# Summing three modulation parts on VectorE in the down stage of the first layer, in a two-layer hybrid decoder trunk

## What is computed

```
c_act = silu(c)
for l in range(2):
    mod = c_act @ ada_w[l] + ada_b[l]              # 1024 x 6144 weights, one row of c
    sh1, sc1, gt1, sh2, sc2, gt2 = split(mod, 6)   # parts 0, 1, 2, 3, 4, 5
    h = rms_norm(x, norm1_g[l]) * (1 + sc1) + sh1
    x = x + gt1 * token_mixer(h, ...)
    h = rms_norm(x, norm2_g[l]) * (1 + sc2) + sh2
    x = x + gt2 * conv_gated_mlp(h, ...)
return rms_norm(x, final_g)
```

## Time and profile before

| what | value |
|---|---|
| median of 3 runs | 1051.32 us (1051.12 to 1051.36) |
| the profiled execution | 1051.65 us, its span 1049.9 us |
| TensorE clock granted, mean | 0.982 |
| busy: PE, DVE, ACT | 94%, 72%, 50% of the span |
| chain that ended last | PE 67%, DVE 17%, issue 10% |
| read from HBM | 199.83 MB, 191 GB/s over the span |

### The profile page before, as it was taken

The page is one execution under the profiler, slowest core; times in us unless marked ns, Lnnn a source line. Parts: engine busy times, 40 slices in busy tenths (PEclk is TensorE's granted clock), DMA queues, the critical chain, the costliest instruction groups (busy, mean ns, idle before and its releaser), DMA issues.

```text
span 1049.9 us, 20436 instructions
## 1 busy us (share of the span) xinstructions
PE 989.0 (94%) x7817; PEld 919.1 (88%) x7817; DVE 751.8 (72%) x1127; ACT 524.6 (50%) x733; POOL 18.0 (2%) x23
## 2 busy tenths in 40 slices
PE   3599999989999999999999999988999999999997
PEld 2498899879888999989898999888988989999997
DVE  2438889996495788876345698999567678788733
ACT  2555355538334555654345544654743466555532
POOL 5000000000000000000000000000000000000001
PEclk8799999999999999999999999999999999999999
DMA  8865545536695354966763545544667635555551
GB/s 303 290 201 163 175 147 183 173 106 214 228 345 177 126 194 163 340 241 240 274 207 98 160 136 170 187 139 153 201 241 279 214 129 183 161 189 173 174 188 41
DMA packets 138952, 202.25 MB, mean 193 GB/s; under 512 B 3416, under 2 KB 114148, under 8 KB 138852
## 3 DMA queue, kind: packets, MB, share of 16 engines
q1 hardware_dynamic: 138501, 200.68, 56.8%
q10 hardware_dynamic: 351, 0.21, 0.1%
HBM read 199.83 MB, written 1.05 MB: 191 GB/s over the span
## 4 chain that ended last, share of the span: by engine, by line
PE 67%; DVE 17%; issue 10%; DMA 2%; SPq 2%; ACT 2%; DVEq 1%; ACTq 0%
PE PB L1280 15%; PE PB L1282 14%; PE PB L1281 14%; DVE wL L862 5%; DVE buf L951 4%; PE SC L1280 2%; PE SC L1281 2%; PE SC L1282 2%; PE MI L1231 2%; DMA raw<-in_w_in 2%; PE PB L1303 1%; DVE rdev L1009 1%; PE ST L1333 1%; DVE cb L1097 1%; PE PB L1304 1%
## 5 line engine op out<-in xcount | busy, mean ns | idle before, releaser
L862 DVE TENSOR_TENSOR wL<-raw,wH 128x2048 fp32r<-128x2048 f32 (+3 forms) x152 | 322.8, 2125 | 120.5 <-ACT wH L606 118.5
L1280 PE MATMUL PB<-hH,wH 128*128 128x256 f32 x1376 | 397.9, 289 | 9.1 <-DVE wL L862 9.1
L1281 PE MATMUL PB<-hL,wH 128*128 128x256 f32 x1376 | 390.6, 284 | 0.0
L1282 PE MATMUL PB<-hH,wL 128*128 128x256 f32 x1376 | 390.5, 284 | 0.0
L606 ACT ACTIVATE wH<-raw 128x2048 fp32r<-128x2048 f32 (+3 forms) x152 | 268.2, 1782 | 121.9 <-DMA raw<-in_w_down 57.8
L1280 PEld LDWEIGHTS PB<-hH,wH 128*128 128x128 f32 x1376 | 265.0, 193 | 24.3 <-issue 13.9
L1281 PEld LDWEIGHTS PB<-hL,wH 128*128 128x128 f32 x1376 | 265.1, 193 | 0.9 <-issue 0.7
L1282 PEld LDWEIGHTS PB<-hH,wL 128*128 128x128 f32 x1376 | 265.2, 193 | 0.0
L951 DVE SCALAR_TENSOR_TENSOR buf<-G,vec,buf 128x256 f32<-128x256 f32 x240 | 98.0, 477 | 0.3
L1303 PE MATMUL PB<-hH,wH 128*128 128x256 f32 x192 | 57.4, 299 | 15.1 <-DVE hL L879 12.3
L1097 DVE SCALAR_TENSOR_TENSOR cb<-PB,vec,cb 128x255 f32<-128x255 f32 (+1 forms) x88 | 36.3, 476 | 32.2 <-ACT cb L753 32.2
(11 more groups left out here) (256 smaller groups left out, 1706.2 us busy)
## 6 DMA issues: line engine op xcount, KB each, us to landing
raw<-in_w_in SPq DMA_DIRECT2D x48, 1024.0 KB, 5.3
raw<-in_w_up SPq DMA_DIRECT2D x44, 1024.0 KB, 5.1
ada<-in_ada_w SPq DMA_DIRECT2D x40, 1024.0 KB, 7.5
raw<-in_w_down SPq DMA_DIRECT2D x22, 1024.0 KB, 4.9
ada_pre<-in_ada_w SPq DMA_DIRECT2D x8, 1024.0 KB, 12.1
raw<-in_w_o SPq DMA_DIRECT2D x8, 1024.0 KB, 8.3
raw<-in_w_out_diff SPq DMA_DIRECT2D x4, 1024.0 KB, 5.1
raw<-in_w_out_conv SPq DMA_DIRECT2D x4, 1024.0 KB, 6.3
```

Of the source, the lines that this page charges most:

```text
L862: dve.tensor_tensor(wL[s][:, 0:size], raw[s][:, 0:size], wH[s][:, 0:size].bitcast(F32), ALU.subtract).then_inc(w_lo[s], 1)
L1280: pe.matmul(out, a, xh(k), start=first and k == 0, stop=False, skip_group_check=True)
L1281: pe.matmul(out, a, xl(k), start=False, stop=False, skip_group_check=True)
L1282: ins = pe.matmul(out, b, xh(k), start=False, stop=last and k == kt - 1, skip_group_check=True)
```

## The change

Three parts of layer 1 (0, 1 and 3) are no longer made by PE's steps. In layer 0's down stage SP loads their twelve chunks (`SUM_LOADS`), DVE multiplies each half of a chunk (128 x 1024) by its scalar of `c_col` and adds it to an accumulator of 128 x 1024 (`ada_sums` at `SUM_STEPS`, 24 instructions, each waiting for the one before), and PE sums over the partitions by eight matmuls with the accumulator as weights and two columns of ones (`reduce_sums`, after chunks 69, 72, 74). ACT has no copy in this. Two accumulators lie over `ca`, `cb` and `th`, `gy`. PE's steps after chunks 61 to 64, 67 to 69 and 71 of layer 0 go, and so do those after 14, 18, 23, 27 of layer 1 with the reduction after 29; in layer 0 these last stay, now under an `If`. The four loads of part 2 of layer 1 stood at steps 71, 72, 73 and 75 of SP; now all stand at step 75, each behind a wait for a sum of DVE that frees its buffer, and ahead of SP's loads of layer 1's first chunks.

```
-ADA_PARTS = [2, 3, 4, 5, 0, 1]
-ADA_GAP, ADA_NEXT, ADA_CHUNKS = 12, 16, 24
-ADA_STEPS = [1, 4, 7, 10, 14, 18, 23, 27, 31, 33, 35, 37] + [None] * 4 + [61, 62, 63, 64, 67, 68, 69, 71]
-ADA_LOADS = [n + 1 for n in ADA_STEPS[:ADA_GAP]] + [39, 40, 42, 41] + [59, 60, 61, 62, 65, 66, 67, 69] + [71, 72, 73, 75]
-ADA_REDUCE_AT = {12: 0, 29: 1, 39: 2, UP + 4 * UP_LOOPS: 3, 65: 4, 73: 5}
+ADA_PARTS = [2, 3, 4, 5]
+ADA_ONCE, ADA_GAP, ADA_CHUNKS = 8, 12, 16
+ADA_STEPS = [1, 4, 7, 10, 14, 18, 23, 27, 31, 33, 35, 37] + [None] * 4
+ADA_LOADS = [n + 1 for n in ADA_STEPS[:ADA_GAP]] + [39, 40, 42, 41]
+ADA_REDUCE_AT = {12: 0, 29: 1, 39: 2, UP + 4 * UP_LOOPS: 3}
+SUM_PARTS = [0, 1, 3]
+SUM_STEPS = [66, 67, 67, 68, 69, 70, 70, 71, 72, 73, 73, 73]
+SUM_LOADS = [59, 60, 61, 62, 70, 71, 71, 72, 73, 74, 74, 75]
+SUM_BUF = [1, 2, 3, 0] * 3
+SUM_REDUCE_AT = {69: 0, 72: 1, 74: 2}
...
+        sums = [ups[:, i:i + 2, :, :].rearrange("p a k t -> p (a k t)") for i in (0, 2)]
...
             def load_ada(l, a):
...
+                if a < ADA_CHUNKS:
+                    sp.wait_ge(ada_used, ADA_FIRST + l * 12 + (a if a < ADA_GAP else a - 3))
+                else:
+                    sp.wait_ge(ada_sum, 2 * (a - ADA_CHUNKS + 9))
...
+            def load_sum(b):
+                part, i = SUM_PARTS[b // ADA_PART], b % ADA_PART
+                if b < ADA_PART:
+                    sp.wait_ge(ada_used, ADA_FIRST + ADA_GAP + b + 1)
+                else:
+                    sp.wait_ge(ada_sum, 2 * (b - 3))
...
+                if n in SUM_LOADS:
+                    with sp.If(l < LAYERS - 1):
+                        for b in range(len(SUM_LOADS)):
+                            if SUM_LOADS[b] == n:
+                                load_sum(b)
+                        if n == CHUNKS - 1:
+                            for i in range(ADA_PART):
+                                load_ada(l, ADA_CHUNKS + i)
...
+            def ada_sums(l, n):
...
+                    for j in ends:
+                        dve.wait_ge(mi_full, 7 + j)
+                        dve.tensor_tensor(mod[:, SUM_PARTS[j] * DT:(SUM_PARTS[j] + 1) * DT], MI[:, 0:2 * DT:2],
...
+                    for b in steps:
+                        part, i = divmod(b, ADA_PART)
+                        acc = sums[part % 2]
+                        dve.wait_ge(ada_in[SUM_BUF[b]], 16 * sum_loads(b))
+                        for k in range(2):
+                            w, c = ada[SUM_BUF[b]][:, k, :], c_col[:, 2 * i + k, 0:1]
+                            if i + k == 0:
+                                if part == 2:
+                                    dve.wait_ge(mi_full, 7)
+                                ins = dve.tensor_scalar(acc, w, c, None, ALU.mult)
+                            else:
+                                dve.wait_ge(ada_sum, 2 * b + k)
+                                ins = dve.scalar_tensor_tensor(acc, w, c, acc, ALU.mult, ALU.add)
+                            ins.then_inc(ada_sum, 1)
...
                 for n in range(DOWN, CHUNKS):
                     if n + 2 < CHUNKS:
                         low(l, n + 2)
-                    ada_work(l, n)
+                    ada_sums(l, n)
...
+            def reduce_sums(j):
+                after(mi_read, 6 + j)
+                after(ada_sum, 2 * ADA_PART * (j + 1))
+                for m in range(DT):
+                    ins = pe.matmul(MI[:, 2 * m:2 * m + 2], sums[j % 2][:, m * P:(m + 1) * P], ones[:, 0:2], start=True,
+                                    stop=True, skip_group_check=True)
+                ins.then_inc(mi_full, 1)
```

More of the change, by code:

```diff
@@ L329, in trunk_kernel @@
         gL = sb("gL", [P, FT, T], F32R, mlp)
[L330 to L333, removed]
+        ups = sb("ups", [P, 4, 2, T], F32, mlp)
+        ca, cb, th, gy = (ups[:, i, :, :] for i in range(4))
+        sums = [ups[:, i:i + 2, :, :].rearrange("p a k t -> p (a k t)") for i in (0, 2)]
         mlp.close()
@@ L363, in trunk_kernel @@
         ada_used, ada_out = sem("ada_used"), sem("ada_rows_out")
+        ada_sum = sem("ada_summed")
         ada_pre_in = [sem(f"ada_pre_in{i}") for i in range(ADA_FIRST)]
@@ L484, in _ @@
                              ada_v[:, 2 * i:2 * i + 2, 1024 * part:1024 * (part + 1)]).then_inc(ada_pre_in[a], 16)
+            def load_sum(b):
[4 more added lines that the diff above has]
+                    sp.wait_ge(ada_sum, 2 * (b - 3))
+                at = SUM_BUF[b]
+                sp.dma_start(ada[at][:, :, :],
+                             ada_v[:, (LAYERS - 1) * DT + 2 * i:(LAYERS - 1) * DT + 2 * i + 2,
+                                   1024 * part:1024 * (part + 1)]).then_inc(ada_in[at], 16)
             def ada_behind(l, n):
[L488 to L491, removed]
+                a = ADA_LOADS.index(n) if n in ADA_LOADS else None
+                if a is not None and a >= ADA_ONCE:
                     load_ada(l, a)
-                else:
+                elif a is not None:
                     with sp.If(l < LAYERS - 1):
                         load_ada(l, a)
+                if n in SUM_LOADS:
[6 more added lines that the diff above has]
+                                load_ada(l, ADA_CHUNKS + i)
             with sp.Fori(0, LAYERS) as l:
@@ L1073, in ada_work @@
                 for at, q in ADA_REDUCE_AT.items():
-                    if at + 1 == n and ADA_PARTS[q] < 2:
+                    if at + 1 == n and q == 1:
                         with dve.If(l < LAYERS - 1):
-                            ada_end(ADA_PARTS[q], l * 6 + 3 + q, vec_all[:, LAYERS - 1, :])
+                            ada_end(ADA_PARTS[q], ada_order(l, q), vec)
                     elif at + 1 == n:
-                        ada_end(ADA_PARTS[q], l * 6 + 3 + q, vec)
+                        ada_end(ADA_PARTS[q], ada_order(l, q), vec)
@@ L1079, in ada_work @@
                         if q == 2:
-                            dve.wait_ge(mi_read, l * 6 + 3 + q)
+                            dve.wait_ge(mi_read, ada_order(l, q))
                             link(dve.scalar_tensor_tensor(gs[:, 1, :], mod[:, 4 * DT:5 * DT], 1.0, vec[:, V_N2:V_N2 + DT],
                                                           ALU.add, ALU.mult))
+            def ada_sums(l, n):
+                steps = [b for b in range(len(SUM_STEPS)) if SUM_STEPS[b] == n]
+                ends = [j for at, j in SUM_REDUCE_AT.items() if at + 1 == n]
+                if not steps + ends:
+                    return
+                with dve.If(l < LAYERS - 1):
+                    for j in ends:
+                        dve.wait_ge(mi_full, 7 + j)
+                        dve.tensor_tensor(mod[:, SUM_PARTS[j] * DT:(SUM_PARTS[j] + 1) * DT], MI[:, 0:2 * DT:2],
+                                          vec_all[:, LAYERS - 1, V_ADAB + SUM_PARTS[j] * DT:V_ADAB + (SUM_PARTS[j] + 1) * DT],
+                                          ALU.add).then_inc(mi_read, 1)
+                    for b in steps:
[12 more added lines that the diff above has]
+                            ins.then_inc(ada_sum, 1)
@@ L1234, in ada_products, with reduce_ada @@
                 ins.then_inc(ada_used, 1)
-            def reduce_ada(part):
-                after(ada_out, part)
+            def reduce_sums(j):
[5 more added lines that the diff above has]
+                ins.then_inc(mi_full, 1)
+            def reduce_ada(evicts):
+                after(ada_out, evicts)
                 for m in range(4):
@@ L1401, in ada_step @@
                 if a % ADA_PART == 0:
-                    after(mi_read, l * 6 + 2 + a // ADA_PART)
+                    after(mi_read, l * 6 + 2 + a // ADA_PART if a < ADA_CHUNKS else 9)
                 ada_products(ada[b], a % ADA_PART)
@@ L1407, in ada_at @@
                 q = ADA_REDUCE_AT.get(n)
-                if q is not None and ADA_PARTS[q] < 2:
+                if q == 1:
                     with pe.If(l < LAYERS - 1):
-                        reduce_ada(l * 6 + 3 + q)
+                        reduce_ada(ada_evicts(l, q))
                 elif q is not None:
-                    reduce_ada(l * 6 + 3 + q)
+                    reduce_ada(ada_evicts(l, q))
+                if n in SUM_REDUCE_AT:
+                    with pe.If(l < LAYERS - 1):
+                        reduce_sums(SUM_REDUCE_AT[n])
                 a = ADA_STEPS.index(n) if n in ADA_STEPS else None
-                if a is not None and ADA_PART <= a < ADA_NEXT:
+                if a is not None and a >= ADA_ONCE:
                     ada_step(l, a)
@@ L1513, in _ @@
                         norm_sum(l, 1)
-                        for a in range(ADA_GAP, ADA_NEXT):
+                        for a in range(ADA_GAP, ADA_CHUNKS):
                             ada_step(l, a)
```

29 lines of the change are left out of this document (17 added, 12 removed).

## The result

The changed kernel took 1055.88 us (median of 5 runs, 1053.73 to 1056.97), the kernel before beside it 1051.32 (5 runs, 1051.03 to 1052.23). The ratio is 1.0041, 95% interval 1.0027 to 1.0056: slower, by more than the 0.2% that a measurement can tell. The forecast was 1051.0 with a range of 1047.0 to 1055.6, and the likeliest answer was "the same". Both are missed, the range by 0.3 us.

The account below looks back on a forecast made before the run. The prediction took PE to bound the kernel, with DVE carrying part of layer 1. From the profiled 1051.65 us, +1.8 at layer 1's start and -2.1 in layer 1 gave 1051.35, with a median of 1051.0; range 1047.0 to 1055.6.

Parts of the forecast that it names:

- What bounds the kernel: Whole kernel: PE nine tenths busy nearly everywhere, DVE with room in layer 0's down stage; DVE carries part of layer 1's chain.
- prices on PE: PE's work: a chunk 5.76 us, a modulation step 1.18, a reduction 0.88, a new narrow reduction 1.65.
- the tail without steps: Layer 0's tail: removed steps and reductions save 10.4 us, three new reductions cost 1.65 each, so PE wins 5.4 us.
- The hand-over: Between the layers: SP held until the last sum delays layer 1's first chunks, giving back 7.2 us, so +1.8 at layer 1's start.
- No stall, but no margin either: Layer 0's tail: DVE's last sums run until 534.3, just ahead of PE's last reduction, due at 534.5.
- The clock: Between the layers: PE idle some 6 us, low clock ahead of the norm's sum with some 2 us of room; zero, -1 to +1.5.
- Layer 1: Layer 1's removed steps: three on DVE's chain give nothing; the step after 27 and reduction after 29 give -2.1 us.
- rival 1: DMA queue in layer 0's tail: serves less, 3.0 us per MB, so +7.3 at layer 1's start, 1056.5 us; chance 0.24.
- my case: The forecast's own case, 1049.3 to 1052.8 us, chance 0.44; chunk 75's weights land at 522.5.
- 2: Layer 1's mixer: the three removed steps there pay too, -3.5 us, 1047.5 us; chance 0.12.
- 3: Between the layers: SP's hold ends early enough that the hand-over is hidden and chunk 75's end decides, 1043.8 us; chance 0.05.
- 4: DMA queue: caught up by chunk 75's weights, landing at 520.6, all behind it 1.9 us earlier, 1049.1 us; chance 0.15.

Follow-up runs that it names:

- With the turn away: The changed kernel with SP's loop over the layers written out as two blocks; 1053.47 us, ratio to before 1.0022.
- the run with the extra matmuls: The changed kernel with 15 unused matmuls of 256 columns on PE between the end of chunk 75 and the sum of squares; 1054.0 us, ratio 1.0025.
- the hold alone: The kernel before with one wait more, SP waiting for the end of chunk 73 before it ends its pass; 1055.38 us, ratio 1.0038.
- the late loads: The changed kernel with part 2's four loads moved behind SP's loads of chunks 0 and 1 of layer 1; 1048.13 us, ratio 0.9972.
- late loads and a late reduction: The changed kernel with part 2's loads behind layer 1's first two chunks and PE's third reduction moved behind chunk 75; 1046.41 us, ratio 0.9946.

## Why the prediction was wrong

**What bounds the kernel, prices on PE, the tail without steps.** Right. The first reduction was due at 502.4 and came at 502.26, for 1.65 us it took 1.68. PE reached E(74) at 534.6 for 534.5. The 5.4 us that PE was to win were there.

**The hand-over** (forecast +1.8, measured +7.2). This is where the sum failed. The forecast had chunk 0 of layer 1 landed at 542.4; it landed at 548.04. These 5.6 us are three terms, rounded:

1. The last sum, 536.45 for 534.3: +2.2. Chunk 75's weights landed at 524.2 for 522.5 (load issued at 515.73, as forecast), and DVE's six operations took 8.02 us for 7.5: 1.28 us each, 1.34 apart, for 1.25. "No stall, but no margin either" was the right warning, and the stall came: PE waited 1.98 us, with the low clock behind it.
2. The fourth `ada_w` load was given 4.9 us to land, the latency of a first transfer; with others ahead of it, it took 5.9 (536.47 to 542.4): +1.0. With the turn away it was 7.0.
3. The chunk was to land 3.0 us behind that load. It landed 5.6 behind: +2.6. This is the step of the mechanism that failed, a wait put at 0.9 us that was over 5: "SP took 0.9 past E(72) before, and I keep that". These 0.9 us were no price of a wait. They were the end of the turn, which had run since 523.8 and was over 0.7 us after E(72); with the loop written out SP took 0.04. With the hold the whole turn comes behind it, and chunk 0 was issued at 542.43, not at 535.3. I had listed what stands behind the waiting instruction in SP's order, but only the loads, and not the end of the loop.

With the turn away the queue kept part of this: the run with the loop written out landed the chunk only 0.9 to 1.6 us earlier and took 2.4 us less in all. The turn and the full queue overlap, and the share of each depends on which is taken away first. What doesn't depend on it is the hold itself: put into the kernel before it costs 4.2 us, and with SP not held at all the changed kernel loses 7.75 us, more than the whole loss.

**The clock** ("zero, from -1 to +1.5"). The size was at its upper end. The sum of squares lost 2.8 us at 0.50, and 1.56 of them stood on the path (the run with the extra matmuls). I had given it 2 us of room ahead of the first `hL`. That room was DVE's turn and its copies of the vectors, and in after DVE's turn doesn't show as a gap at all: the copy at 557.73 stands 0.1 behind `low(1,1)`. The loop's own line shows why:

```profile
L1214 DVEq COMPARE_BRANCH  x1: 63/63/63, 553.1 to 553.1; - x1
L1214 DVEq FUSED_REGOPS  x1: 74/74/74, 557.6 to 557.6; - x1
```

DVE's sequencer, with no wait in the adds, had run ahead of the engine: it jumped at 553.1, while the engine was still at the adds, and was back at 557.6, when `low(1,1)` ended. In before the jump was at 547.7, at the last adds, and the next instruction at 551.8, 1.4 us behind `low(1,1)`. In the sum the two cancel: what the low clock added, the hidden gap of 1.48 us gave back.

**Layer 1** (forecast -2.1). Right at its place. The chain in layer 1's mixer, first of before, then of after:

```profile
743.33 1.73 PE ST L1333 x8
...
762.69 0.99 PE MI L1231 x8
```
```profile
738.10 1.99 PE ST L1416 x8
748.32 1.73 PE ST L1416 x8
766.88 0.99 PE MI L1305 x8
```

From the sum at 731.91 to 743.33, across the step after chunk 27, were 11.42 us and are 10.22: -1.20 for a forecast of -1.18. To 762.69, across the reduction after 29, were 19.36 and are 18.56: -0.80 for -0.88. The three other steps gave 0.3 to 0.6 by the run that puts them back. All of the remaining 0.95 of 2.95 lies ahead of 731.91. Before ran chunk 0 of layer 1 partly at 0.50 of the clock; after had 1.00 from 560 us on, as its low stretch lay earlier, under the sum of squares. That this accounts for the rest is my reading, and untested. From the reciprocal to the reduction before has 393.93 us, but before with SP's loop written out 392.74, and with the hold alone 392.73: the part moves by 1 us on its own, so that the gain is 1.8 to 2.95.

**The queue, rival 1.** It gave 1056.5 and stands nearest to the time, but not for its reason. It wanted 3.0 us per MB; the stretches from 500 to 522 moved 389 to 414 GB/s, 2.5 to 2.7 us, but for one of 176 (342 followed from 522 to 524). The sum loads are issued only when DVE frees a buffer (511.85 and 514.56), and the three transfers behind chunk 74 took 9.1 us, not 7.7. So chunk 75's weights came midway between my case and the rival's (522.5, 526.3), by gaps and small losses and not by a lower rate throughout. The Trainium skill's page DMA: Bandwidth & Descriptors, section Bandwidth, gives 358 GB/s as what binds, and says in the same section that it is each core's share when both cores of the pair load at once. The trace, of one core at work, has 389 to 414 GB/s in every stretch of 2 us from 500 to 510 and from 512 to 522 us, so that limit did not bind there.

**Rivals 2, 3 and 4.** 2 fell (0.3 to 0.6 us for three steps). 3 needed an earlier end of the hold. Its price, 1043.8 for a hidden hand-over, is near the 1043.18 us of the version without the hold and with all loops written out; as that version has other terms in it, the nearness shows nothing. 4 needed chunk 75's weights at 520.6. The range failed on its upper side since no case held SP's turn, and since it ended at 1055.6, short of rival 1's own 1056.5. Of the signs, the sharpest was the right one: the load of chunk 0 "at about 535" went out at 542.43. The wait of PE for the last sum, 1.98 us, stayed just under the 2 us that were to mean "slower".

## What to carry to other kernels

When a wait is put at the end of an engine's pass through a loop, the turn of that loop stands behind it; look for the idle stretch in which the turn was hidden so far, and price it with the queue as full as it will be then (2.5 us or 5 to 6 here). Put loads for which nobody is in a hurry behind those for which somebody waits, and the wait for a slow sum where the engine has no other work behind it. A stall of PE can be paid twice: with the late loads, once for the wait of 1.99 us and once for the clock behind it, a reduction of 3.30 us in place of 1.70.

## What the runs showed of the hardware

- The turn of SP's loop: 2.46 us with an idle DMA queue; 5.0 to 6.1 with a megabyte or more under way, in the code of before and of after alike. ACT's: 2.7 with the queue at 16 GB/s or less, 5.2 with it at 338 to 349 for the first 3 us. Instruction packets show on the same DMA engines.
- Of a turn only the part shows that nothing hides: DVE's was 4.1 us with a gap of 1.48 in before, 4.5 with none in after, 6.0 with a gap of 3.98 in the version with late loads and a late reduction; ACT's 5.2 with one of 3.49, once DVE's was gone. With the loops written out the gaps are gone.
- Writing SP's loop out where no turn was on the path gave nothing: 0.14% slower, 0.04 to 0.23%, which is at the edge of what these runs can tell from no change.
- Dependent scalar_tensor_tensor operations of 1024 columns on DVE: 1.28 us each, 1.34 apart.
- Behind a wait of PE of 1.98 us and a reduction of sixteen matmuls of two columns the granted clock stood at 0.55 and 0.60 for 4 us; behind a wait of 0.53 us and the same reduction at 0.50 for 2 us and 0.68 for the next 2.
